# Gate stage: VectorE turns the first two column groups of the scaled residual, and the gate's products move one weight piece later

## What is computed

```python
# first_block, after the feed-forward
gate = jax.nn.sigmoid(rms_norm(h, norm_ple[i]) @ ple_w_gate[i])
h = h + (p[i] @ ple_w_proj[i]) * gate
...
x = rms_norm(h, norm_final)
# second_block
h = rms_norm_2(x, norm_g[i, 0])
q, k, v = h @ w_in            # v first in this kernel
```

## Time and profile before

| | us |
|---|---|
| median of three runs | 2202.08 (2201.79 to 2202.5) |
| the profiled execution | 2202.45 |
| its span in the trace | 2200.6 |
| PE busy | 2188.3 (99%) |
| DVE busy | 1517.5 (69%) |
| ACT busy | 1123.5 (51%) |
| POOL busy | 628.7 (29%) |

### The profile page before, as it was taken

One profiled execution on the slowest core, in us unless ns is written; L12 is line 12 of the kernel. 1 busy time (PEld: TensorE's weight loads), 2 busy tenths in 40 slices (PEclk: granted clock), 3 DMA queues, 4 the chain that ended last, 5 costly groups with the idle time before them and its releaser, 6 DMA issues.

```text
span 2200.6 us, 34123 instructions
## 1 busy us (share of the span) xinstructions
PE 2188.3 (99%) x11565; PEld 1870.8 (85%) x11565; DVE 1517.5 (69%) x2075; ACT 1123.5 (51%) x1690; POOL 628.7 (29%) x573
## 2 busy tenths in 40 slices
PE   9999999999999999999999999999999999999998
PEld 8888988888888888888888887888888888888887
DVE  6877765558658757755966666577774688756875
ACT  6445555555445445454556455465553455434553
POOL 3202320361362363153000133006540255303431
PEclk9999999999999999999999999999999999999999
DMA  7665335456555556555555653545555555555554
GB/s 253 232 228 170 107 133 187 169 185 213 189 186 206 191 181 209 201 200 191 186 187 192 220 174 134 198 157 187 194 191 194 188 191 191 191 191 191 189 209 147
DMA packets 118079, 414.28 MB, mean 188 GB/s; under 512 B 12897, under 2 KB 18049, under 8 KB 117473
## 3 DMA queue, kind: packets, MB, share of 16 engines
q1 hardware_dynamic: 111600, 401.37, 53.2%
q10 hardware_dynamic: 6384, 11.70, 1.7%
HBM read 409.29 MB, written 2.15 MB: 187 GB/s over the span
## 4 chain that ended last, share of the span: by engine, by line
PE 93%; POOL 2%; issue 2%; DVE 2%; ACT 1%; DMA 0%; POOLq 0%; DVEq 0%; ACTq 0%
PE bank L547 31%; PE bank L555 16%; PE bank L1207 4%; PE bank L1205 4%; PE bank L1206 4%; PE bank L881 4%; PE bank L882 4%; PE bank L883 4%; PE bank L605 3%; PE bank L606 3%; PE bank L604 3%; POOL bias L2544 1%; PE bank L660 1%; PE bank L661 1%; PE bank L662 1%
## 5 line engine op out<-in xcount | busy, mean ns | idle before, releaser
L1246 DVE TENSOR_TENSOR wboth<-raw,wboth 128x1024 fp32r<-128x1024 f32 x756 | 963.9, 1279 | 542.1 <-ACT wboth L2049 541.0
L2049 ACT CAST wboth<-raw 128x1024 fp32r<-128x1024 f32 x756 | 780.4, 1041 | 585.6 <-PE bank L1207 126.5
L547 PE MATMUL bank<-A,wboth 128*128 128x512 f32 x2928 | 705.4, 392 | 0.5 <-DVE wboth L1246 0.3
L547 PEld LDWEIGHTS bank<-A,wboth 128*128 128x128 f32 x2928 | 536.9, 188 | 105.2 <-issue 1.2
L555 PEld LDWEIGHTS bank<-A,wboth 128*128 128x128 f32 x2928 | 376.7, 191 | 14.8
L555 PE MATMUL bank<-A,wboth 128*128 128x256 f32 x2928 | 384.0, 283 | 0.0
L2544 POOL TENSOR_TENSOR PT<-z,rs 128x256 f32<-128x256 f32 x88 | 73.4, 835 | 465.8 <-DVE z L1277 465.2
L2544 POOL TENSOR_TENSOR bias<-z,rs 128x256 f32<-128x256 f32 x64 | 104.5, 1633 | 199.1 <-DVE z L1277 109.7
L1277 DVE TENSOR_REDUCE z<-bank 128x256 f32<-128x512 f32 x172 | 118.0, 687 | 28.2 <-PE bank L547 27.9
L1205 PE MATMUL bank<-wboth,H 128*128 128x512 f32 x352 | 136.9, 389 | 0.0
L1206 PE MATMUL bank<-wboth,H 128*128 128x512 f32 x352 | 136.9, 389 | 0.0
(11 more groups left out here) (340 smaller groups left out, 3090.3 us busy)
## 6 DMA issues: line engine op xcount, KB each, us to landing
raw<-wstream SPq DMA_DIRECT2D x756, 512.0 KB, 3.3
bias<-bias_rows ACTq DMA_DIRECT2D x6, 512.0 KB, 6.1
x<-xrows ACTq DMA_DIRECT2D x1, 2048.0 KB, 10.6
bias<-grows ACTq DMA_DIRECT2D x2, 1024.0 KB, 7.2
out<-x SPq DMA_DIRECT2D x8, 256.0 KB, 2.1
x<-xT SPq DMA_DIRECT2D x7, 256.0 KB, 5.4
pA<-bias_rows ACTq DMA_DIRECT2D x2, 512.0 KB, 8.8
Sm<-grows ACTq DMA_DIRECT2D x1, 1024.0 KB, 6.7
```

Of the source, the lines that this page charges most:

```text
L547: last = nc.tensor.matmul(bank(j)[:, :], whi[:, s, cols(i)], moving(j, k), start=(k == 0), stop=(k == K - 1))
L1246: V.tensor_tensor(wlo[:, s, 0:w], raw[:, s, 0:w], whi[:, s, 0:w].bitcast(F32), ALU.subtract).then_inc(lo_ready, 1)
L2049: C.copy(whi[:, s, 0:w], raw[:, s, 0:w]).then_inc(hi_ready, 1)
```

## The change

VectorE now turns groups 0 and 1 of the gate's columns: `gate_turn(f, i)` makes quarter i (four L1373-type instructions) at step 8f+9+i, one quarter behind each of four splits. TensorE loses `turn_gate(0)` and `turn_gate(1)`; `turn_gate(2)` moves from after piece 3 to after piece 4 of group 3; `turn_gate(3)` stays in v2. For groups 0 and 1 ScalarE and VectorE read the turned columns from `z` instead of the banks. `gate_in(f)` moves from step 8f+7 to step 8f+8, so it now follows the split of piece 8f+11. `gate_squares`, `gate_hi` and `gate_lo` all move by one step.

```diff
             for f in range(4):
                 rows_group(PB["gate"] + 8 * f, PB["gate"] + 8 * f, UB["gate"] + 2 * f, UB["gate"] + 2 * f, DT, A,
-                           lambda k: (a2_ready, k + 1), {3: lambda: turn_gate(f - 1)} if f else {0: lambda: turn_fd(3)})
+                           lambda k: (a2_ready, k + 1), {0: {0: lambda: turn_fd(3)}, 3: {4: lambda: turn_gate(2)}}.get(f, {}))
...
-            def turn_quarters(f, i0, turned):
+            def turn_quarters(f, i0, turned, n=2):
-                for i in (i0, i0 + 1):
+                for i in range(i0, i0 + n):
...
+            def gate_turn(f, i):
+                if i == 0:
+                    dve.wait_ge(ple_gain, 2 * f + 2)
+                if f and i == 0:
+                    dve.wait_ge(a3_ready, 4 * f)
+                turn_quarters(f, i, ple_turned, 1)
             def gate_lo(f):
-                tiles_lo(H, "g0", f, ple_hi, a3_ready)
+                if f < 2:
+                    turned_lo(H, "g0", f, ple_hi, a3_ready)
+                else:
+                    tiles_lo(H, "g0", f, ple_hi, a3_ready)
             dve.wait_ge(in_gf, 16)
-            rows_body(PB["gate"], PB["gate"], 8, 4, gate_in,
-                      {2: lambda: fd_lo(3), 3: norm_gate, **{8 * f + 5: lambda f=f: gate_lo(f - 1) for f in range(1, 4)}})
+            rows_body(PB["gate"], PB["gate"], 32, 1, lambda f: None,
+                      {2: lambda: fd_lo(3), 3: norm_gate, **{8 * f + 8: lambda f=f: gate_in(f) for f in range(4)},
+                       **{8 * f + 9 + i: lambda f=f, i=i: gate_turn(f, i) for f in range(2) for i in range(4)},
+                       **{8 * f + 6: lambda f=f: gate_lo(f - 1) for f in range(1, 4)}})
...
             def gate_hi(f):
-                tiles_hi(H, "g0", f, ple_turned, ple_hi)
+                if f < 2:
+                    turned_hi(H, "g0", f, ple_turned, ple_hi)
+                else:
+                    tiles_hi(H, "g0", f, ple_turned, ple_hi)
...
-                **{8 * f + 2: lambda f=f: gate_squares(f - 1) for f in range(1, 4)},
-                **{8 * f + 4: lambda f=f: gate_hi(f - 1) for f in range(1, 4)}})
+                **{8 * f + 3: lambda f=f: gate_squares(f - 1) for f in range(1, 4)},
+                **{8 * f + 5: lambda f=f: gate_hi(f - 1) for f in range(1, 4)}})
```

## The result

The median went from 2202.13 us (21 runs) to 2205.59 us (21 runs): 3.46 us slower, a ratio of 1.0016 with a 95% interval of 1.001 to 1.0022, or 2.2 to 4.8 us. That is less than 0.2%. The profiled execution took 2206.56 us, with a span of 2204.8 us; 0.8 us of its distance to the profiled execution before arose ahead of the stage: the turn that follows gate piece 0, which the change doesn't touch, begins at 1107.22 in it and at 1106.44 in the trace before.

What follows compares the result with a forecast made beforehand. TensorE, 99% busy, was taken as the bound, so work leaving it is gained and its waits are lost. -1.76 + 3.89 + 1.28 = +3.41 us gave 2205.5 us against the median, own range 2205.0 to 2206.0, wider range 2201.5 to 2207.5.

Steps and rivals of the forecast that it cites:

- What TensorE loses: Gate stage: two turns of eight transposes, 0.88 us each, leave TensorE's queue, a gain of 1.76 us.
- What VectorE gets: Gate groups 0 and 1: a split with a quarter costs 3.01 us; VectorE's round is 23.92 us against TensorE's 21.79.
- two prices: A split with one quarter costs 2.95 or 3.07 us, by whether a wait stands ahead of the quarter.
- The waits up to piece 28: Gate stage: TensorE waits 3.89 us for VectorE, two rounds each 2.13 us behind, less 0.37 us of slack.
- The move of `gate_in(3)`: Put behind split 35, it makes `turn_gate(3)` in v2 wait 1.28 us with the hand-over.
- What I counted at nothing: `gate_squares` a step later, the freed banks, and `turned_lo` in place of `tiles_lo`: no cost.
- Sum: Whole kernel: -1.76 + 3.89 + 1.28 = +3.41 us, giving 2205.5 us.
- VectorE keeps up: Rival: VectorE's gate round is no longer than 21.8 us; 2201.6 us (chance 0.12), or 2200.3 (0.05).
- slower rival: Slower by over 0.2% if a split with its quarter costs 3.13 us or more; 2207.0 at 3.20; chance 0.24.
- slack at piece 12: Gate stage: split 12 is done at 1136.84, TensorE wants it at 1137.25, leaving 0.37 us after hand-over.

Runs made afterwards that it cites:

- halves kernel: The change with gate_in(0) to gate_in(2) split over steps 8f+7 and 8f+8, gate_in(3) at step 31, gate_hi at 8f+6: 2200.62 us against 2202.48 before.
- the copies later: The change with ScalarE's copies gate_hi at step 8f+6 instead of 8f+5: 2203.41 us against 2202.50 before the change.
- the products back: The change with all four gate_in put back to step 8f+7: 2205.64 us against 2202.34 before the change.
- both edits: The change with all four gate_in at step 8f+7 and gate_hi at 8f+6: 2201.65 us against 2202.34 before the change.

## Why the prediction was right, point by point

- **What TensorE loses.** 1.76 us for two turns. The halves kernel, with hardly another loss, is 1.80 us shorter by its trace and 1.9 us by its median.
- **What VectorE gets.** Round 23.92 us forecast, 23.96 and 23.95 us in the trace (1132.30, 1156.26, 1180.21). A split with a quarter took 2.94 us with the first quarter and 3.07 to 3.08 us with the other three, 12.17 us for four against 12.04: three of the four seams are the dearer one. My reason for the two prices, a wait ahead of the first quarter, was wrong: in the first group of fd3 `fd_turn` waits ahead of both its calls, and the seams are 1.14 and 1.25 us all the same. The cheap seam is always that of quarter 0, whose 32 rows are the first, where the split's begin too; why it is cheaper no run here shows. From the fourth quarter's end (1146.75 + 1.80 = 1148.55) to split 17 (1151.26) it is 2.71 us against 2.73.
- **The waits up to piece 28.** 3.89 us forecast, 3.98 measured, most of it at the pieces named: "0.8 us of it in pieces 14 to 16", then 20 and 28. I said "about 1 us at piece 20 and again at piece 28"; the idle times there are 0.96 and 0.97 us, 1.29 us at 14 to 16, and 0.3 to 0.5 us at each of 21 to 24, which I had not named.
- **The move of `gate_in(3)`.** 1.28 us forecast, 1.40 us of idle time measured, and 1.37 us when done alone.
- **What I counted at nothing.** The squares, the freed banks and the other form of `gate_lo` show no wait of TensorE; without the transposes all the rest of the change costs only the wait in v2.
- **Sum.** 3.41 us forecast; 3.58 us in the stage, 3.46 us between the medians. That the round came out within 0.04 us is partly luck: the four splits with a quarter were 0.13 us dearer than I took them, the rest of the round 0.09 us cheaper. So is the match of the medians within 0.1 us, since their interval is 2.2 to 4.8 us; the mechanism is borne out by the waits, not by that match. The loss, which I had put under what a measurement can tell from no change, is clear of it.
- **The rivals.** That VectorE keeps up is out: with the transposes gone from VectorE the waits are gone. The seams of the slower rival cost 3.08 us at most, below its 3.13.
- **What the prediction did not see.** It took the slack at piece 12 as the one that counts. In the change's order it is; the three misses among my later expectations (the copies later, the products back, both edits) show that the rule is another: TensorE waits for the latest split of the round against its own piece, and the candidates are the first split behind each long step. Nor did it see that the round could be made to fit with the steps that there are.

## What to carry to other kernels

Before work is moved from a saturated engine to a half idle one, add up the round of the receiving engine, with the waits of its partners in it, and compare it with the round of the saturated one: 69% busy on the page was 15.1 of 22.7 us in this stage, and still 7.2 us of transposes made a round of 24.0 us against 21.8. What decides is then the worst piece, not the mean: place the long steps so that no split stands behind two of them, and put a waiting copy behind the cast that the next engine needs. Here the same two groups on VectorE cost 3.5 us in one order and gained 1.9 us in another.

## What the runs showed of the hardware

In the kernel with the products back, the second wait of TensorE was followed by a stretch at half speed. TensorE's timeline there (start, duration):

```profile
1182.24 0.47 PE L604 MATMUL bank<-wboth,A 128*128 128x512 f32 x1 [1.93 <-DVE wboth L1246]
...
1183.39 0.63 PE L605 MATMUL bank<-wboth,A 128*128 128x512 f32 x1
1183.81 0.63 PE L606 MATMUL bank<-wboth,A 128*128 128x512 f32 x1
1184.24 0.63 PE L604 MATMUL bank<-wboth,A 128*128 128x512 f32 x1
...
1186.66 0.40 PE L604 MATMUL bank<-wboth,A 128*128 128x512 f32 x1
1186.90 0.40 PE L605 MATMUL bank<-wboth,A 128*128 128x512 f32 x1
```

From 1183.0 to 1186.4 matmuls start 0.43 us apart instead of 0.23: the lower of the clock's two levels, 1.2 instead of 2.4 GHz, and some 1.6 us lost. The busy time by stretch shows it in the granted clock (column ahead of the DMA share), 0.83 over these 10 us:

```profile
1182.00:1192.00 10.00, 9.76 (x40) 7.96 (x41) 5.96 (x6) 5.28 (x13) 0.00 (x0) 0.83 0.77 259
```

TensorE had waited 2.3 us just before, and 2.0 us some 24 us earlier. The same kernel was profiled once more (d_again):

> The kernel with gate_in put back to step 8f+7 once more, for its trace alone: TensorE's waits of 2.0 and 2.3 us at pieces 19 and 27 should repeat. If the fall of the granted clock to its lower level behind the second of them (some 3.5 us long, 1.6 us lost) comes from these waits, it is there again; if it was chance, it isn't.

The waits were there again, 2.01 and 2.30 us, but the clock stayed at 1.00 in that stretch:

```profile
1182.00:1192.00 10.00, 8.58 (x42) 7.19 (x43) 7.13 (x7) 7.08 (x15) 0.00 (x0) 1.00 0.71 249
```

From the turn behind piece 0 to that in v2 it is 97.04 us in it, 2.28 us more than before, the 2.3 us that the waits alone explain. So the waits don't bring the fall every time. Yet the mean granted clock of this run was 0.998 too: the fall lies near its start, where TensorE had been busy for 1.4 of the 3 us before:

```profile
6.00:9.00 3.00, 1.40 (x7) 1.10 (x8) 1.44 (x4) 2.06 (x5) 0.00 (x0) 0.96 1.02 388
9.00:12.00 3.00, 3.00 (x9) 2.32 (x8) 2.82 (x6) 3.00 (x6) 0.00 (x0) 0.50 1.03 371
```

The trace of the change, also 0.998, has its fall at the same place (0.51). So the mean says that TensorE ran slowly somewhere, not where. Over 11 runs it was 0.998 in nine for the kernel with the products back, and in one to three of the 11 runs of each other kernel of the experiments, so this kernel seems to have a fall more often than the others; that it comes in this stage, and from the waits, was seen in one trace of two and is not shown. In the trace of the change, with the same 4 us of waiting in pieces of at most 1 us up to piece 28, the clock was 1.00 in every stretch of the stage.
